# Expert routing from unscaled rows, and output copies issued later, in a one-layer decoder step

## What is computed

```python
h = rmsnorm(x, g_mix)                     # combined projection -> q, k, v, u
x = x + W_out([dilated window attention(q, k, v, cached windows) | causal pooling(u)])
x = x + cross_attention(rmsnorm(x, g_x), 256 memory tokens)
h = rmsnorm(x, g_ff)                      # mixture of experts: top 4 of 32
logits = h @ w_router + b_router
top_v, top_i = top_k(logits, 4); gates = softmax(top_v)
# expert e, on its own tokens:  hu = h @ w_gate_up[e] + b_gate_up[e]
#   a = g * sigmoid(1.702 g) * (u + 1)   (g, u clamped);  y = a @ w_down[e] + b_down[e]
x = x + sum of gate * y over the four experts
y = rmsnorm(x, g_final)
# also returned: the key and value windows, moved on by four rows, 8 sequences x 2044 kept rows x 512 each
```

## Time and profile before

| | us |
|---|---|
| median of 3 runs | 1411.29 |
| lowest, highest run | 1403.95, 1412.52 |
| the profiled execution | 1409.75 |
| its span in the profile | 1408.0 |
| TensorE busy | 1255.7 |
| VectorE busy | 481.2 |
| ScalarE busy | 230.3 |
| GpSimd busy | 67.7 |
| moved by DMA | 557.14 MB, mean 396 GB/s |

### The profile page before, as it was taken

The page is one execution under the profiler, slowest core; times in us unless marked ns, Lnnn a source line. Parts: engine busy times, 40 slices in busy tenths (PEclk is TensorE's granted clock), DMA queues, the critical chain, the costliest instruction groups (busy, mean ns, idle before and its releaser), DMA issues.

```text
span 1408.0 us, 16530 instructions
## 1 busy us (share of the span) xinstructions
PE 1255.7 (89%) x6407; PEld 528.5 (38%) x6407; DVE 481.2 (34%) x1037; ACT 230.3 (16%) x448; POOL 67.7 (5%) x69
## 2 busy tenths in 40 slices
PE   7989877989897999998999989999899998999986
PEld 5444323456644433333333333333333333333332
DVE  2387888332326412312232122321223212132124
ACT  1334443211311110110110100110011010011102
POOL 2010000005007000000000000000000000000000
PEclk9999988999997999999999999999999999999998
DMA  9999999998989699999999999999999999999993
GB/s 339 353 381 363 399 397 379 361 370 306 360 354 344 254 431 427 427 429 426 429 428 429 429 429 429 428 430 427 430 427 430 427 429 428 429 429 429 429 428 158
DMA packets 51740, 557.14 MB, mean 396 GB/s; under 512 B 7021, under 2 KB 9301, under 8 KB 15885
## 3 DMA queue, kind: packets, MB, share of 16 engines
q1 hardware_dynamic: 50629, 553.04, 96.0%
q0 software_dynamic: 1072, 3.57, 0.6%
HBM read 552.02 MB, written 71.72 MB: 443 GB/s over the span
## 4 chain that ended last, share of the span: by engine, by line
DMA 55%; PE 35%; DVE 5%; ACT 2%; issue 1%; SPq 1%; DVEq 0%; ACTq 0%; PEldq 0%
DMA wide<-in_w_gate_up 49%; PE bank L1954 12%; DMA wide<-in_cache_v_win 3%; PE bank L1642 3%; PE bank L1983 2%; PE bank L1684 2%; PE bank L1749 2%; PE bank L1512 2%; PE bank L1508 1%; PE bank L1662 1%; DMA slim<-in_w_xq 1%; DMA slim<-in_w_xv 1%; ACT wide L787 1%; PE bank L1737 1%; PE bank L1791 1%
## 5 line engine op out<-in xcount | busy, mean ns | idle before, releaser
L1954 PE MATMUL bank<-wide,att 128*64 128x512 f32 x2048 | 463.3, 596 | 58.5 <-DMA wide<-in_w_gate_up 58.3
L1954 PEld LDWEIGHTS bank<-wide,att 128*64 128x64 f32 x2048 | 139.3, 136 | 362.5 <-issue 228.8
L1983 PE MATMUL bank<-slim,att 128*64 128x512 f32 x1024 | 226.8, 595 | 0.0
L1422 DVE TENSOR_SCALAR att<-bank 128x512 f32<-128x512 f32 x32 | 22.1, 691 | 469.0 <-PE bank L1954 469.0
L1983 PEld LDWEIGHTS bank<-slim,att 128*64 128x64 f32 x1024 | 70.6, 137 | 152.2 <-issue 149.2
L1401 DVE TENSOR_TENSOR x<-x,bank 128x512 f32<-128x512 f32 x68 | 46.6, 685 | 233.1 <-PE bank L1936 226.4
L980 ACT ACTIVATE att<-att 128x512 f32<-128x512 f32 x32 | 20.2, 630 | 517.6 <-DVE att L1422 517.6
L1936 PE MATMUL bank<-tb,att 128*128 128x512 f32 (+1 forms) x192 | 84.7, 611 | 1.8 <-ACT tb L989 1.3
L989 ACT ACTIVATE tb<-bank 64x512 f32<-64x512 f32 x64 | 37.8, 591 | 234.1 <-PE bank L1983 233.7
L1662 PE MATMUL bank<-slim,ta 128*128 128x512 f32 x128 | 57.8, 601 | 0.5 <-DMA slim<-in_w_xv 0.3
L1176 DVE TENSOR_REDUCE small<-wide 128x24 f32<-128x1536 f32 x28 | 49.1, 1753 | 1.0
(11 more groups left out here) (290 smaller groups left out, 1153.1 us busy)
## 6 DMA issues: line engine op xcount, KB each, us to landing
wide<-in_w_gate_up SPq DMA_DIRECT2D x128, 2048.0 KB, 25.4
slim<-in_w_down SPq DMA_DIRECT2D x64, 2048.0 KB, 22.0
out_k_win_sample<-in_cache_k_win SPq DMA_DIRECT2D x16, 2044.0 KB, 25.3
out_v_win_sample<-in_cache_v_win SPq DMA_DIRECT2D x16, 2044.0 KB, 22.9
wide<-in_w_in SPq DMA_DIRECT2D x8, 1024.0 KB, 15.8
wide<-in_cache_v_win SPq DMA_DIRECT2D x8, 1024.0 KB, 7.5
wide<-in_cache_mem_k SPq DMA_DIRECT2D x8, 1024.0 KB, 24.4
wide<-in_cache_mem_v SPq DMA_DIRECT2D x8, 1024.0 KB, 14.7
```

What stands on the lines that cost most here:

```text
L1954: ins = M(bk[half[h], :], rows[:, k, :], wide[:, k, c:c + 512], start=False, stop=k == KC - 1)
L1983: ins = M(bank_y[half[h], :], aT[:, f % 4, f // 4, :], slim[:, f, 512 * h:512 * h + 512], start=f == 0, stop=f == KC - 1)
```

## The change

- `COPIES` becomes 6, 1, 2, 1, 1, 1, 1, 1, 2, 2, 4, 2, 2, 3 (from 5, 1, 3, 1, 2, 2, 2, 2, 2, 2, 3, 2, 1, 3); three pieces instead of one are left for behind expert 0.
- The identity and x1 are loaded from ScalarE's queue; the bias product "toep" comes ahead of ten small products.
- In the attention loop the wait for the late value rows moves behind the first two kinds of value products, and VectorE's wait for the late key rows to the third part of its first product.
- Routing: TensorE transposes the rows of x as they are, with a step of eight floats, so the transposes don't wait for the norm. The inverse norm and the router's bias, loaded to all partitions, are applied to the logits by one VectorE operation. ScalarE writes the scaled rows to `hn`. Tile 1 is handled in two halves of 64 channels per block: squares, transposes, gain and router products of the first half come ahead of the second half of the "xo" product. The one-hot compares of tiles 0 and 2 come ahead of the last table.
- ScalarE makes the bfloat16 parts of tile 1, GpSimd only subtracts. The first four inner blocks of expert 0 need only the first half of the gathered rows.

```diff
-        COPIES = [5, 1, 3, 1, 2, 2, 2, 2, 2, 2, 3, 2, 1, 3]
+        COPIES = [6, 1, 2, 1, 1, 1, 1, 1, 2, 2, 4, 2, 2, 3]
...
-            load(sp, "ident", ident[:, :], i["c_ident"])
-            for t in (0, 2, 1):
+            for t in (0, 2):
...
-            load(sp, "brow", brow, i["b_router"])
+            load(sp, "brow", brow, bass.AP(i["b_router"].tensor, 0, [[0, P], [1, EXPERTS]]))
...
+            for part in range(2):
+                for h in range(2):
+                    c = slice(512 * h, 512 * h + 512)
+                    pool.wait_ge(bf_in, 2 * part + h + 1)
+                    src = hn[:, 1, c] if part == 0 else rest[:, c]
+                    nc.gpsimd.tensor_tensor(rest[:, c], src, hparts[1][:, part, c], ALU.subtract).then_inc(left_in, 1)
...
+            load(act, "ident", ident[:, :], ident_rows)
+            load(act, "x1", x[:, 1, :], second_rows)
             act.wait_ge(consts, 2)
...
+            def scaled_rows(t, n, ks):
+                return A(hn[0:n, t, :].rearrange("n (k p) -> n k p", p=P)[:, ks, :], x[0:n, t, :].rearrange("n (p k) -> n k p", k=KC)[:, ks, :],
+                         ACT.Copy, scale=stat[0:n, 16 + t:17 + t])
...
+            act.wait_ge(scale_in, 1)
+            scaled_rows(0, P, slice(0, KC)).then_inc(rows_in, 1)
...
+            read_out(act, "xo", 1, 0)
+            A(hn[:, 1, 0:512], x[:, 1, 0:512], ACT.Square, accum_out=meansq[:, 17:18]).then_inc(early_sum, 1)
+            read_out(act, "xo", 1, 1)
+            link(A(hn[:, 1, 512:D], x[:, 1, 512:D], ACT.Square, accum_out=meansq[:, 36:37]))
...
+            act.wait_ge(scale_in, 3)
+            for h in range(2):
+                c = slice(512 * h, 512 * h + 512)
+                link(scaled_rows(1, P, slice(4 * h, 4 * h + 4)))
+                A(hparts[1][:, 0, c], hn[:, 1, c], ACT.Copy).then_inc(bf_in, 1)
+            for part in (1, 2):
+                for h in range(2):
+                    c = slice(512 * h, 512 * h + 512)
+                    act.wait_ge(left_in, 2 * (part - 1) + h + 1)
+                    A(hparts[1][:, part, c], rest[:, c], ACT.Copy).then_inc(bf_in, 1)
...
+                    if t == 0:
+                        dve.wait_ge(late_k, b + 1)
                     V.tensor_tensor(pd[:, 2, :], kw[:, 8, :], ps[:, :], ALU.mult).then_inc(s, 1)
...
-                dve.wait_ge(late_k, b + 1)
...
-                V.tensor_copy(logit[0:n, t, :], ps[0:n, 0:EXPERTS]).then_inc(s, 1)
+                V.scalar_tensor_tensor(out=logit[0:n, t, :], in0=ps[0:n, 0:EXPERTS], scalar=stat[0:n, 16 + t:17 + t], in1=brow[0:n, :],
+                                       op0=ALU.mult, op1=ALU.add).then_inc(s, 1)
...
+            residual("xo", 0)
+            scale_of(0, P, 9)
+            residual("xo", 2)
+            gained("tr3", tb, gff, (0,))
+            scale_of(2, NS, 10)
             residual("xo", 1, (0,))
+            dve.wait_ge(early_sum, 1)
...
             largest(0)
             gained("tr3", tb, gff, (2,))
+            largest(2)
+            gained_half(0)
+            slots(0)
+            tile_onehot(0, 0)
             residual("xo", 1, (1,))
+            dve.wait_ge(squares, 11)
...
+            gained_half(1)
+            largest(1)
             slots(2)
...
+            tile_onehot(0, 2)
+            slots(1)
+            tile_onehot(0, 1).then_inc(onehot_in, 2)
...
+            ps, s = take(pe, "toep")
+            M(ps[0:HEADS, 0:TOEP], rb, cb[:, 0:TOEP], start=True, stop=True).then_inc(s, 1)
             for kind in range(6):
...
-                pe.wait_ge(late_v, b + 1)
...
-                for k, kind in enumerate((2, 0, 1, 3)):
+                for k, kind in enumerate((0, 1, 2, 3)):
+                    if kind == 2:
+                        pe.wait_ge(late_v, b + 1)
...
+            def turned_rows(t):
+                t0, n = TOK[t]
+                src = x[0:n, t, :].rearrange("n (p k) -> n k p", k=KC)
...
+            def turned_half(h):
+                src = x[:, 1, :].rearrange("n (p k) -> n k p", k=KC)
+                for kh in range(2):
+                    ps, s = take(pe, "tr3", 1, h, kh)
+                    for c in range(4):
+                        rows = src[:, 4 * kh + c, 64 * h:64 * h + 64]
+                        out = ps[64 * h:64 * h + 64, P * c:P * c + P]
+                        ins = M(out, rows, ident[:, :], start=True, stop=True) if h else TR(out, rows, ident[:, :])
+                    ins.then_inc(s, 1)
...
             rows_times("xo", 0, ta, P, 0)
             rows_times("xo", 2, ta, NS, SEQ)
+            read_out(pe, "xo", 0, 0), read_out(pe, "xo", 0, 1)
+            turned_rows(0)
             tile1 = [take(pe, "xo", 1, 0)]
             half_times(0, range(KC))
-            transposes("tr3", 5, (0,))
+            pe.wait_ge(loaded["wr"], 16)
+            route(0)
+            read_out(pe, "xo", 2)
+            turned_rows(2)
             tile1.append(take(pe, "xo", 1, 1))
             half_times(1, range(KC // 2))
+            route(2)
+            read_out(pe, "xo", 1, 0)
+            turned_half(0)
+            pe.wait_ge(loaded["before"], 16)
+            position(0)
             half_times(1, range(KC // 2, KC))
...
+            route1 = take(pe, "route", 1)
+            route_half(0)
+            position(2)
+            read_out(pe, "xo", 1, 1)
+            turned_half(1)
+            route_half(1)
             position(1)
...
-                pe.wait_ge(xe_in, n + 2)
+                pe.wait_ge(xe_in, 1 if first and i == 0 else n + 2)
...
+                    if k == 4 and first and i == 0:
+                        pe.wait_ge(xe_in, 2)
```

More of the change, by code:

```diff
@@ L729, in _ @@
             pool.wait_ge(hparts_in, 1)
[L730 to L740, removed]
+            for part in range(2):
[4 more added lines that the diff above has]
+                    nc.gpsimd.tensor_tensor(rest[:, c], src, hparts[1][:, part, c], ALU.subtract).then_inc(left_in, 1)
+            pool.wait_ge(left_in, 4)
             pool.wait_ge(stored["kv"], 64)
@@ new lines, in _ @@
+            ins.then_inc(tall, 1)
+            read_out(act, "xo", 1, 0)
+            A(hn[:, 1, 0:512], x[:, 1, 0:512], ACT.Square, accum_out=meansq[:, 17:18]).then_inc(early_sum, 1)
+            read_out(act, "xo", 1, 1)
+            link(A(hn[:, 1, 512:D], x[:, 1, 512:D], ACT.Square, accum_out=meansq[:, 36:37]))
+            act.wait_ge(early_root, 1)
+            A(stat[:, 17:18], meansq[:, 36:37], ACT.Sqrt, bias=stat[:, 36:37], scale=1.0 / D).then_inc(squares, 1)
+            act.wait_ge(scale_in, 3)
@@ new lines, in tile_onehot, with pair_onehot @@
+            def tile_onehot(n, t):
+                for a in range(2):
+                    ins = V.tensor_scalar(onehot[0:MROWS[t], t, CAP * a:CAP * a + CAP], iota[0:MROWS[t], 0:CAP],
+                                          table[0:MROWS[t], t, ds(n + a, 1)], None, ALU.is_equal)
+                return ins
+            def pair_onehot(n):
+                for t in range(3):
+                    ins = tile_onehot(n, t)
+                ins.then_inc(onehot_in, 2)
+            residual("xo", 0)
@@ L1847, in route, with route_half @@
                 for k in range(KC):
-                    M(ps[0:n, 0:EXPERTS], tb[:, k, t0:t0 + n], wr[:, k, :], start=k == 0, stop=False)
-                M(ps[0:n, 0:EXPERTS], ones[0:1, 0:n], brow, start=False, stop=True).then_inc(s, 1)
+                    ins = M(ps[0:n, 0:EXPERTS], tb[:, k, t0:t0 + n], wr[:, k, :], start=k == 0, stop=k == KC - 1)
+                ins.then_inc(s, 1)
+            def route_half(h):
+                read_out(pe, "tr3", 1, h, 0), read_out(pe, "tr3", 1, h, 1)
+                for k in range(KC):
+                    ins = M(route1[0][:, 0:EXPERTS], tb[64 * h:64 * h + 64, k, P:2 * P], wr[64 * h:64 * h + 64, k, :],
+                            start=h == 0 and k == 0, stop=h == 1 and k == KC - 1)
+                if h:
+                    ins.then_inc(route1[1], 1)
             def half_times(h, ks):
@@ L1885, in _ @@
             pe.sem_inc(slim_used, 1)
-            route(2)
-            pe.wait_ge(loaded["before"], 16)
-            position(0), position(2)
-            transposes("tr3", 6, (1,))
-            route(1)
+            route1 = take(pe, "route", 1)
[4 more added lines that the diff above has]
+            route_half(1)
             position(1)
@@ L1911, in _ @@
                 read_out(pe, *name)
-            pe.wait_ge(hparts_in, 3)
+            pe.wait_ge(bf_in, 6)
             gather(0, 1, bank_t)
```

93 lines of the change are left out of this document (49 added, 44 removed).

## The result

The changed kernel takes 1411.5 us (median of 20 runs, 1408.7 to 1415.9); the kernel before, in 20 runs beside them, 1407.5. The ratio is 1.0036 (95% interval 1.0024 to 1.0049): 4 us slower, where 5 us faster was forecast. The size is within the 1% named in the forecast, but twenty runs a side tell it from no change.

What follows compares the result with a forecast made beforehand. The prediction took the DMA engines to bound the kernel, the end set by when expert loads run without a break. From 1409.75 us, minus 4.3 (loop) and 1 (routing), it got 1404.4, said 1404; range 1394 to 1415.

Steps and rivals of the forecast that it cites:

- the 1% named in the forecast: Whole kernel: the measurement tells about 1%, 14 us, from no change; chance of landing within it 0.76.
- the sixth piece, "0 at the end": Ahead of key window 1: one more piece delays it 4.9 us (0 to 6.7), absorbed by later waits.
- the 9 us wait that was counted as cover: Attention loop: ScalarE's 8.98 us wait for value window 1, expected with 2.1 us more to absorb the 4.9 us.
- the second rival: Attention loop: sixth piece's 4.9 us delay stays, tail pieces 4 us late; 1418.7, or 1415 with one; chance 0.12.
- its own sign: Attention loop: the slower rival decides if the third batch's scores come later than before.
- What the loop gives back, 4.3 us: Attention loop: four pieces fewer, so value windows no longer come last; saves 4.3 us (0 to 11.4).
- The routing, 6 us, hidden behind the copies: Routing before expert 0: shortened by 6 us (0 to 10), but moved pieces fill the 11.6 us DMA hole.
- The early sum's wait: Routing: VectorE's new wait holds up the first tile's top-4 and what follows, about 1 us, within the 6.
- The fourth rival: Routing: longer by over the 7 us cover (strided transposes, ScalarE's list); 1409 with 5 beyond; chance 0.14 with nothing.
- Strided transposes: Routing: if transposes of x with a 32-byte step stretch 1.5 times, it saves about 4 us instead of 6.
- The front, counted 0: Kernel start: x1 and identity from ScalarE's queue save 1 us (0 to 2.6), counted 0 because key window 1 follows.
- The transition, -1 (-3 to +4): Routing into expert 1's load: 1.2 us of DMA idle time after 468 goes; net -1 us (-3 to +4).

Runs made afterwards that it cites:

- e4: The kernel before with only the sixth piece moved ahead of key window 1 (list starts 6, 1, 2 instead of 5, 1, 3); ratio 1.0035.
- e3: The changed kernel with five pieces instead of six ahead of key window 1 (list starts 5, 1, 3); ratio 1.0000.
- e8: The kernel before with only the list of copies replaced by that of e3; ratio 0.9992.
- e1: The kernel before with only the change's new list of copies; ratio 1.0035.
- e6: The changed kernel with four pieces instead of six ahead of key window 1 (list starts 4, 1, 4); ratio 1.0013.
- e13: The kernel before with only the list of copies replaced by that of e9; ratio 0.9957.
- e9: The changed kernel with copies 4, 1, 2, 1, 2, 2, 2, 2, 2, 2, 4, 2, 2, 3; ratio 0.9938.
- e2: The changed kernel with the old list of copies; ratio 0.9989.
- e10: e2 with the last residual ahead of the first tile's slots and one-hot in VectorE's routing order; ratio 0.9988.
- e11: e10 with VectorE's early-sum wait moved from ahead of the first tile's top-4 to just ahead of the last residual; ratio 0.9971.
- e14: e12 with GpSimd's second step of tile 2's parts held back until the last tile's scale is done; ratio 0.9918.
- e15: e12 with the identity and x1 loaded from SyncE's queue again; ratio 0.9889, 1393.6 us beside 1408.6.
- e12: The changed kernel with e9's copies and e11's two moves in VectorE's routing order; ratio 0.9908, 1390.7 us beside 1403.9.

## Why the prediction was wrong, step by step

**The step that failed: the sixth piece, "0 at the end".** Three things in it. First, its price was taken at 4.9 us, the row of pieces beside loads; it measured 6.4 to 6.9 in four pairs of kernels that differ in it alone (before and e4, e3 and after, e8 and e1, e6 and e3). The queue ahead of key window 1 is full and moves at the other rate; the kernel before:

```profile
60.00:75.00 15.00, 10.76 (x81) 6.56 (x76) 13.67 (x47) 6.82 (x15) 1.15 (x2) 0.77 0.97 315
```

2.09 MB at 315 GB/s are 6.6 us. Where the queue runs dry, as in e13, a piece fewer gives only 3.8. Second, the delay grew: TensorE was idle for 12.0 us, its granted clock was at the lower of its two levels (0.50) from 95 to 105 us, and the work from row(1, 0) to the second scores took 27.7 us at 0.82 (after) where before it took 24.2 at 1.00; the two rows, after then before:

```profile
103.83:131.54 27.71, 25.13 (x109) 13.86 (x109) 18.77 (x29) 17.37 (x44) 3.39 (x5) 0.82 0.92 352
```

```profile
97.51:121.69 24.18, 20.87 (x109) 10.75 (x110) 18.77 (x29) 16.94 (x44) 3.38 (x5) 1.00 1.01 375
```

In e4, the piece alone, 6.7 us at the window became 9.5 at the second scores. That this growth comes of the idle stretch is not shown: in e9 TensorE waits no longer than 2.3 us at a time there, and the same work takes 26.8 us at a clock of 0.87. Third, the cover was there, as the forecast said, but not all of it: the waits at value window 1 and behind took back 6.8 of these 9.5 by the eighth scores (252.2 against 249.4). And the 9 us wait that was counted as cover is no free time: it is the loop's second gate, and e9 shows that it could be removed instead of filled.

So the second rival came true in kind, by its own sign (the third batch's scores come 9.9 us later), though the delay doesn't stay: in e4 2.8 us are left at the eighth scores, and in after 4.0. That its 4.9 us for the front is what e4 measures (0.35% of 1406, with an interval from 2 to 8 us) is luck in part: the piece cost more at the window, and a part was taken back.

The piece is not the whole of the miss. e3 has the change without it, with a DMA share of 0.91 in the first 250 us and no hole, and takes the time of before: 1.0000 (0.9986 to 1.0015), where the forecast's 1404.4 of 1409.75 is 0.996. The terms below that failed are the routing and the transition.

**What the loop gives back, 4.3 us:** right as a stretch. From the second to the eighth scores e3 takes 4.1 us less than e2, e8 3.9 less than before. In the changed kernel this and the catching up are one: 121.9 against 127.7 us. In the launch little of it is left: e8, the lighter loop alone, measures 0.9992 (0.9970 to 1.0013); e8's eighth scores come 3.2 us earlier, and the moved pieces cost some 2 us at the tail (below).

**The routing, 6 us, hidden behind the copies:** wrong. It saves 5.1 us at the tail, but the term left out that VectorE, with the first tile's slots and one-hot (each stretched by GpSimd to 1 to 2 us) ahead of the last residual, reaches it 4.8 us late. The early sum's wait is 3.83 us long, since ScalarE scales two tiles (4.2 us) and copies rows (2.1) ahead of that square; moving it brings the residual from 41.4 us behind xo (e10) to 39.9 (e11), so its cost is near the 1 us forecast. Over five kernels with the old routing xo to expert 0 takes 65.1 us on the mean (64.3 to 65.9), over seven with the new 64.5 (63.4 to 65.5). Nothing was hidden: in e2 the old list leaves a DMA share of 0.81 over the same 71 us counted from xo (388.3 to 459.3), and the time is that of before. The fourth rival looked for the loss in ScalarE's list and the transposes. In the traces it is VectorE's order and its conflict with GpSimd: with the order changed (e10, e11) the residual comes 3.4 and 4.9 us earlier than in e2, counted from xo, and expert 0 only 1.2 and 1.6, since the conflict moves into the scale. What that is worth in time is not clear of noise.

The rule on shared ports would have warned of it. The Trainium skill, page SBUF — State Buffer, section "Who interferes with whom", says that a VectorE instruction with two SBUF inputs contends with a GpSimd instruction that reads SBUF, that one in a two-port mode contends with GpSimd too, and that the ports they share are an exclusive lock. The trace of e11 agrees on the first: such operations end with GpSimd's (1.78 us against 0.16 in e14), the one-input operation at 435.13 keeps its 0.15. Larger one-input operations stretch as well (line 1350 in the changed kernel, 1.05 us against 0.18 at rest); that they run in such a mode no run here shows.

**Strided transposes:** the ratio 1.5 that the forecast weighed is seen in the small tile and not in the large one, all at a granted clock of 1.00. Eight of 128 rows take 1.16 us in e3, eight contiguous ones 1.04 in e8; eight of 32 rows, e3 then e8:

```profile
418.96 1.06 PE L1907 MATMUL bank<-ident,x 32*128 32x32 f32 x8
```

```profile
429.74 0.65 PE L1473 MATMUL bank<-ident,hn 32*128 32x32 f32 x8
```

That is 0.5 us for these two tiles, far less than the 2 that the forecast allowed for. ScalarE's scaling with that step stretches most, 2.10 us against 1.06 for its square of the same shape.

**The front, counted 0:** right within the noise (e15), though the first scores came 5.5 us earlier.

**The transition, -1 (-3 to +4):** sign wrong, size within. From expert 0's start to the end, the seven kernels with the new list's tail take 947.5 us on the mean (945.9 to 949.7), the five with the old one 945.4 (944.9 to 945.9): the pieces moved to the tail cost 2.1 us.

Left open: how much of e9's gain over e13 belongs to waits and routing, and what a routing without the conflict of VectorE and GpSimd would give; no such order was tried.

## What to carry to other kernels

- In a queue that doesn't run dry, price a moved transfer at the rate of its own stretch, and ask for each later load what stands ahead of it; a wait that would absorb the delay is itself a gate to remove.
- Read the granted clock beside the duration of a stretch: here the same work took 24.2 us at 1.00 (before) and 26.3 to 27.7 us at 0.78 to 0.87 (after, e1, e3, e4, e9, e10 and e12).
- When work is moved ahead of a step on an in-order engine, compare the time at which that step's input is ready with the time at which the engine gets there.

## What the runs showed unexpectedly

- A 2.09 MB copy that takes 4.9 us of DMA time elsewhere delays a load behind it by 6.4 to 6.9 us in a full queue, and by 3.8 where the queue runs dry (e13).
- VectorE's operations on a single column with two inputs take 0.16 us alone and up to 1.78 beside GpSimd.
- The half transposes in the form of products (16 instructions) take 3.61 us in the changed kernel at 448.35, the other half's eight transposes 1.09 at 437.98. Much of that is the clock: it is 0.53 there and 1.00 at the other half, and before, eight transposes of full size took 1.97 us at 0.50 and 1.04 at 1.00.
